# Two blocks of a network on one core: the second block's projections and gates as one stage of seven block products, kept in DRAM

## The chip, the cores and the metric

One NeuronCore of a Trainium2 chip. Its engines: TensorE (PE; weight loads are shown apart, as PEld), VectorE (DVE), ScalarE (ACT), GpSimd (POOL), and SyncE (SP), which here only issues transfers. A ScalarE row marked ACTq is a transfer that ScalarE issues. The metric is the device time of one launch, in microseconds (us), a median over runs.

## The reference, cut to what matters

`x` has 1024 tokens and 1024 features, in fp32. A first block (mLSTM, window attention, a gated convolutional feed-forward part) is followed by a second one, on which the change works:

```
xn   = rmsnorm_2(x, attn_norm_g)
proj = xn @ w_in                        # 1024 x 4864
u_pool, qkv_dil, qkv_sb, u_s5 = ...     # 512 + 2304 + 1536 + 512 columns
y_pool = pool_mixer(u_pool)             # running means over 2, 4, 8, 16 tokens, then 128x128 products
y_dil  = dilated_attention(qkv_dil)     # 3 groups of 4 heads, dilation 1, 4, 16, relative bias
y_sb   = stick_breaking_attention(qkv_sb)   # 4 heads of 128
y_s5   = s5_mixer(u_s5)                 # a state-space scan, gelu, a gated product
for bi, yb in enumerate((y_pool, y_dil, y_sb, y_s5)):
    gate   = sigmoid(xn @ w_gate[bi])   # 1024 x 1024 each
    merged = merged + gate * (yb @ w_branch[row:row + width])
x = x + merged @ w_out                  # then a feed-forward part and a last norm
```

So `xn` is multiplied by 38 column tiles of `w_in` (128 columns each) and by 32 of `w_gate`.

## The kernel before

**Dense products.** Every fp32 operand of a dense product is split into a rounded part and a rest, `hi` and `lo`; one product is three matmuls of 128x128 by 128x512: hi hi, lo hi, hi lo. Activations lie feature-major: 8 tiles of 128 features by 1024 tokens, in two halves of 512 tokens. A column tile of weights against all of `xn` takes 8 x 2 x 3 = 48 matmuls. The up and down products of both feed-forward parts save an eighth of that: they take a 2x2 block form of Winograd's, with seven block products instead of eight, at the price of sums of weights and operands before and sums of products after.

**The second block's stages.** The down product of the first block (`seven_down`, L1867) ends with the norm that makes `xn`: VectorE scales (L2053), ScalarE rounds (L1976), VectorE makes the rests (L2057). Three stages follow, each a block of its own, with a barrier at its end:

1. `pool_and_dilated` (L3132). A dense `Stream` (L2951) makes 30 column tiles: u for the pooling, q, k and v of the three dilated groups, v of the stick-breaking heads, and q, k of two of its heads. SyncE loads weights in half tiles of 256 KB (L2986), three in flight; GpSimd rounds them (L3004) and makes the rests (L3006); TensorE multiplies (L3041); ScalarE and VectorE empty the banks. v is turned from feature-major to token-major on TensorE as it comes (L3027). Beside it runs the "side" work. The relative bias is summed in the first steps and stored 12 times, once a head, from one partition to 128 skewed rows in DRAM (`bias_scratch<-xT`, 192 KB each, issued by ScalarE, L3464). SyncE reads it back as bias tiles (L3525) as soon as the four stores of a group have landed. The pooling chain runs on VectorE, with one product a group (L3266). Then the three groups, 8 blocks each: TensorE scores (L3282), VectorE bias (L3379) and maximum (L3384), ScalarE exponentials, TensorE turns (L3293) and outputs (L3305). Two groups' rows go through DRAM (`dil_scratch`) to be reordered; a mixing step (L3447, L3449) weighs the groups.
2. `stick_branch` (L3587). A second `Stream` of 8 column tiles beside 48 units of attention, one of up to 512 query columns each: logits (L3653), ScalarE's log of the remainder (L3719 to L3726), VectorE, a cast and a rest on GpSimd (L3752, L3754), products with triangular matrices that sum over later keys (L3668, L3670, L3681, L3682), the output (L3690).
3. `merge` (L4121). By a list of steps, per half of the tokens, half of the output features and branch: 8 weight tiles of the gate and 2 or 4 of the branch, 12 matmuls each (L4423); sigmoid on ScalarE (L4190), gate times product on VectorE (L4214), addition on GpSimd (L4329). The S5 scan's pieces stand at fixed steps (L4354, L4365, L4368, L4385). The gate weights are read, rounded and split once for each half of the tokens.

**What sets the order.** Each engine runs its own instruction list in the order in which it was written; semaphores tie the lists together. In stages 1 and 2 a list of booleans decides, for every engine alike, whether the next piece is the stream's or the side's:

```
def woven(order, stream, side):
    for own in order:
        next(stream if own else side, None)
```

`spread` (L3111) makes that list, an even mixture of the stream's slots (of 8 matmuls) and the side's steps.

Of the kernel before, what the change touches and what calls it, by code (L numbers as in the profile page):

```python
# [33 lines left out]
BRANCH_AT = 214976  # L34
# [221 lines left out]
def build(nc, io):  # L256
    with ExitStack() as ctx:
# [15 lines left out]
        with ExitStack() as s1:  # L273
# [12 lines left out]
            with ExitStack() as s2:  # L286
# [12 lines left out]
            branches = Stream(c, "px", branch_jobs(io), xn[0], xn[1], 2, None, at=BRANCH_AT)  # L299
            branches.ident = ident[:, :]  # L300
            down1, ahead, xn_saved, finish = seven_down(
                c, "down1", io["w_down"][0], xT, lambda k: ada[:, 40 + k, 0:1], (xT, saved[0]), xn,
                c.vec[:, 2, 96:112].rearrange("p (j k) -> p j k", j=2), (gains[:, 2, :], gains[:, 3, :]),
                (xT, saved[1]), branches, kept, up1.lead)
            down.append(down1)
            in_one_block(nc, (mix, up1, down1))
            ahead += [xn_saved, finish]
        second_block(c, io, xT, ident, ones, gains, s5, xn, hid, h, saved, branches, ahead, kept)
# [1558 lines left out]
def seven_down(c, name, w, x, gate, first, h, gain, outer, save, ahead, kept, lead):  # L1867
# [19 lines left out]
    total, weighted, r1, r12, root = (lambda half, j=j: cell(((41, 42, 43, 35, 36), (32, 33, 34, 37, HEAD))[half][j]) for j in range(5))  # L1887
# [63 lines left out]
    def scalar(act):  # L1951
# [52 lines left out]
        if h is not None:  # L2004
            for k in range(DK):
                rounding(1, k)
# [6 lines left out]
    def vector(dve):  # L2013
# [205 lines left out]
    def finish_store(act):  # L2219
        act.wait_ge(outer_made, 2 * DK)  # L2220
        act.dma_start(save[1][:, :, RIGHT], save[0][:, :, RIGHT]).then_inc(saved[1], 16)

    return Programs(sync, scalar, vector, gpsimd, tensor, split_hi, split_lo, scaled), begun, saved, (finish, finish_store)
# [632 lines left out]
SB_E = 128  # L2856
O_POOL, O_DIL, O_SB, O_S5 = 0, 512, 2816, 4352
# [11 lines left out]
def second_block(c, io, xT, ident, ones, gains, s5, xn_pair, hid, h, saved, branches, ahead, kept):  # L2869
    nc = c.nc  # L2870
    if True:
        with ExitStack() as s1:
            c.sb("xn_room", [P, 2 * DK * T], s1)
            xn_hi, xn_lo = xn_pair[0], xn_pair[1]
            yT = c.sb("yT", [P, Y_TILES, T], s1)
            w_in = io["w_in_2"][0].rearrange("(k p) n -> p k n", p=P)
            with ExitStack() as s2:
                pool_and_dilated(c, io, branches, ahead, yT, xT, ident, s2)
            c.end_stage()
            with ExitStack() as s2:  # L2880
                stick_branch(c, io, w_in, xn_hi, xn_lo, yT, xT, ident, ones, s5["u"], s2)
            c.end_stage()
            with ExitStack() as s3:
                merged, lead = merge(c, io, s5, xn_hi, xn_lo, yT, xT, s3)
        second_feed_forward(c, io, xT, ident, gains, hid, h, saved, kept, merged, lead)


def second_feed_forward(c, io, xT, ident, gains, hid, h, saved, kept, merged, lead):
# [5 lines left out]
    down2, _, _, _ = seven_down(c, "down2", io["w_down_2"][0], xT, None, (xT, saved[2]), None,  # L2894
# [1658 lines left out]
```

## Time and profile before

| | |
|---|---|
| three runs | 3680.94, 3684.49, 3688.26 us; median 3684.49 |
| span of the profiled execution, from its first to its last instruction | 3678.0 us |
| busy in the span | PE 93%, PEld 74%, DVE 54%, ACT 34%, POOL 30% |
| stage 1, 1588 to 2047 us | PE busy 440.95 of 459 |
| stage 2, 2052 to 2256 us | PE busy 195.74 of 204 |
| stage 3, 2256 to 2892 us | PE busy 603.74 of 636 |

The page gives the span of the profiled execution; launch and end around it are in the runs' times only. Busy times are sums over instructions; matmuls are pipelined, so that the mean duration of one (about 0.4 us) is longer than the pitch at which they follow one another. A line of a group gives after the bar the busy time, the mean of one instruction, and the idle time of the engine just before them with what ended it.

### The profile page before, as it was taken

Reading aid. Unit: us, or ns where it says so; the run is one execution under the profiler, and the core shown is the slowest. Engines: PE = TensorE matmul, PEld = TensorE weight load, DVE = VectorE, ACT = ScalarE, POOL = GpSimd, SP = SyncE. Lnnn points to the kernel's source line nnn. Section 1 sums busy time; section 2 is a strip of 40 time slices with the busy share of each in tenths; the row PEclk is TensorE's granted clock in tenths of the full one; section 3 lists DMA queues with packets and bytes.
Section 4 is the critical chain, followed back from the end, with each engine's and each line's share of the span. In section 5 each row is a group of like instructions: output and inputs, shape, how many; then the busy total and the mean of one; then the engine's idle time right before and its main releaser. Section 6 shows DMA issues by size and latency. Waiting matters only on the chain. (4 is left out here: it accounts for less than half of the span.)

```text
span 3678.0 us, 44316 instructions
## 1 busy us (share of the span) xinstructions
PE 3424.0 (93%) x16719; PEld 2726.2 (74%) x16719; DVE 2002.8 (54%) x2809; ACT 1251.9 (34%) x2205; POOL 1101.5 (30%) x950
## 2 busy tenths in 40 slices
PE   5799998988999999879999898999999989999998
PEld 3577777866788888767888676775777767888886
DVE  5346654556867768833335443542434466555586
ACT  3523333144333344411223354231333333222343
POOL 4122112213655510222222453551111135444111
PEclk7799999999999999989999999999999999999999
DMA  8611112032333346238111112442222423333552
GB/s 255 230 54 44 58 46 101 36 119 87 98 101 103 109 170 202 72 83 74 50 46 50 30 29 77 123 134 69 92 92 93 162 82 108 96 108 101 197 184 95
DMA packets 317982, 373.41 MB, mean 102 GB/s; under 512 B 30254, under 2 KB 225166, under 8 KB 316986
## 3 DMA queue, kind: packets, MB, share of 16 engines
q1 hardware_dynamic: 307880, 342.29, 29.3%
q10 hardware_dynamic: 3490, 11.35, 2.6%
q0 software_dynamic: 6400, 16.94, 1.8%
q8 instruction: 134, 2.20, 0.2%
q14 instruction: 78, 0.64, 0.1%
HBM read 283.58 MB, written 86.28 MB: 101 GB/s over the span
## 5 line engine op out<-in xcount | busy, mean ns | idle before, releaser
L2348 POOL TENSOR_TENSOR up_w_lo<-up_w_sum,up_w_hi 128x512 fp32r<-128x512 f32 x176 | 248.4, 1440 | 326.3 <-ACT up_w_hi L2324 324.5
L4250 DVE TENSOR_TENSOR mg_w_lo<-mg_raw,mg_w_hi 128x512 fp32r<-128x512 f32 x184 | 153.4, 836 | 208.5 <-ACT mg_w_hi L4178 208.0
L2348 POOL TENSOR_TENSOR up_w_lo<-up_raw,up_w_hi 128x512 fp32r<-128x512 f32 x132 | 201.4, 1541 | 129.3 <-ACT up_w_hi L2324 129.3
L4178 ACT CAST mg_w_hi<-mg_raw 128x512 fp32r<-128x512 f32 x184 | 115.1, 626 | 354.1 <-PE ps L4423 173.2
L1920 ACT CAST down_hi<-down_room 128x1024 fp32r<-128x1024 f32 x154 | 161.0, 1051 | 210.7 <-PE ps L2200 131.7
L1924 DVE TENSOR_TENSOR down_lo<-down_room,down_hi 128x1024 fp32r<-128x1024 f32 x154 | 192.1, 1253 | 71.4 <-ACT down_hi L1920 70.2
L3041 PE MATMUL ps<-xn_hi_at,px_w_hi 128*128 128x512 f32 x480 | 193.5, 403 | 32.5 <-PEq L1507 17.9
L2324 ACT CAST up_w_hi<-up_w_sum 128x512 fp32r<-128x512 f32 x176 | 99.7, 614 | 323.4 <-DVE up_w_sum L2337 323.4
L762 PE MATMUL ps<-h_hi,stream_hi 128*128 128x512 f32 (+1 forms) x488 | 185.3, 380 | 24.7 <-POOL stream_lo L737 17.4
L2554 PE MATMUL ps<-h_hi_at,up_w_lo 128*128 128x512 f32 x704 | 191.6, 394 | 16.0 <-POOL up_w_lo L2348 16.0
L2554 PE MATMUL ps<-h_hi_at,up_w_hi 128*128 128x512 f32 x704 | 192.9, 396 | 7.2 <-ACT up_w_hi L2324 7.2
L3041 PE MATMUL ps<-xn_hi_at,px_w_lo 128*128 128x512 f32 x480 | 191.9, 400 | 0.0
L3041 PE MATMUL ps<-xn_lo_at,px_w_hi 128*128 128x512 f32 x480 | 191.3, 399 | 0.0
L2554 PE MATMUL ps<-h_lo_at,up_w_hi 128*128 128x512 f32 x704 | 190.8, 393 | 0.0
L762 PE MATMUL ps<-h_hi,stream_lo 128*128 128x512 f32 (+1 forms) x488 | 184.7, 379 | 0.0
L762 PE MATMUL ps<-h_lo,stream_hi 128*128 128x512 f32 (+1 forms) x488 | 183.8, 377 | 0.0
L2200 PE MATMUL ps<-down_hi 128*128 128x512 f32 x616 | 167.0, 393 | 3.5 <-ACT down_hi L1920 3.5
L4329 POOL TENSOR_TENSOR xT<-xT,sig 128x512 f32<-128x512 f32 x48 | 67.6, 1408 | 342.7 <-DVE sig L4214 336.7
L2554 PEld LDWEIGHTS ps<-h_hi_at,up_w_lo 128*128 128x128 f32 x704 | 133.8, 191 | 45.4 <-POOL up_w_lo L2348 17.7
L2200 PE MATMUL ps<-down_hi,down_lo 128*128 128x512 f32 x616 | 165.5, 391 | 0.0
L2200 PE MATMUL ps<-down_lo,down_hi 128*128 128x512 f32 x616 | 165.5, 391 | 0.0
L2554 PEld LDWEIGHTS ps<-h_hi_at,up_w_hi 128*128 128x128 f32 x704 | 134.0, 191 | 37.8 <-ACT up_w_hi L2324 8.9
(598 smaller groups left out, 8018.1 us busy)
## 6 DMA issues: line engine op xcount, KB each, us to landing
up_raw<-in_w_up SPq DMA_DIRECT2D x88, 512.0 KB, 5.2
down_room<-hid_kept SPq DMA_DIRECT2D x154, 256.0 KB, 2.9
mg_raw<-in_w_gate SPq DMA_DIRECT2D x128, 256.0 KB, 2.7
hid_kept<-up_out SPq DMA_DIRECT2D x44, 512.0 KB, 3.6
down_room<-in_w_down SPq DMA_DIRECT2D x88, 256.0 KB, 4.3
px_raw<-in_w_in SPq DMA_DIRECT2D x60, 256.0 KB, 3.0
mg_raw<-in_w_branch SPq DMA_DIRECT2D x56, 256.0 KB, 2.7
wa<-in_w_ada SPq DMA_DIRECT2D x12, 1024.0 KB, 9.9
```

Source lines behind the costliest of these rows:

```text
L762: ins = nc.tensor.matmul(ps[:, self.bank + q % 2, 0:size], w[:, i % 2, k * P:(k + 1) * P], r[:, k, at:at + size], start=(x == 0), stop=(x ...
L1920: nc.scalar.copy(hi[:, u % R], both(u)).then_inc(hi_made, 1)
L1924: nc.vector.tensor_tensor(lo[:, u % R], both(u), hi[:, u % R].bitcast(F32), ALU.subtract).then_inc(rest_made, 1)
L2200: ins = nc.tensor.matmul(bank(q, j), a[:, u % R, n, j * P:(j + 1) * P], b[:, u % R, 1 - n, :], start=(k == 0 and r == 0), stop=(k == KH - ...
L2324: nc.scalar.copy(w_hi[:, s, :], source(t, i)).then_inc(hi_made, 1)
L2348: nc.gpsimd.tensor_tensor(w_lo[:, s, :], source(t, i), w_hi[:, s, :].bitcast(F32), ALU.subtract).then_inc(lo_made, 1)
L2554: ins = nc.tensor.matmul(bank(t, i), wp[:, s, k * P:(k + 1) * P], op[:, k], start=(r == 0 and k == 0), stop=(r == 2 and k == H - 1))
L3041: ins = nc.tensor.matmul(ps[:, half, :], w[:, n % 2, k * P:(k + 1) * P], x[:, 4 * kh + k, half * BANK:(half + 1) * BANK], start=(kh == 0 a ...
L4178: nc.scalar.copy(w_hi[:, s, :], w_raw[:, s, :]).then_inc(hi_ready[s], 1)
L4250: nc.vector.tensor_tensor(w_lo[:, s, :], w_raw[:, s, :], w_hi[:, s, :].bitcast(F32), ALU.subtract).then_inc(lo_ready[s], 1)
L4329: nc.gpsimd.tensor_tensor(target(i, m), target(i, m), sig[:, m, :], ALU.add).then_inc(added, 1)
```

## The change

A new stage, `project_all`, stands between the down product and stage 1. It makes all 70 column tiles that multiply `xn` (38 projections, 32 gates) in 35 pairs, each pair by seven block products of 12 matmuls. VectorE makes the weight sums and the sums of products, ScalarE rounds weights and applies sigmoid, scale or S5's order of steps, GpSimd makes the rests. The results are stored to DRAM, two tiles of 512 KB a pair. The list of pairs, the operands and TensorE's program:

```diff
+def projection_pairs(io, proj, gates, u_dram):
...
+    starts += [O_SB + 1024 + h * P for h in range(4)] + [O_SB + h * P for h in (0, 1, 4, 5, 2, 3, 6, 7)]
+    kinds = ["plain"] * len(starts)
+    kinds[SB_TILE] = kinds[SB_TILE + 1] = kinds[SB_TILE + 4] = kinds[SB_TILE + 5] = "scale"
+    tiles = [(w_in[:, :, at:at + P], kind, proj[:, i, :]) for i, (at, kind) in enumerate(zip(starts, kinds))]
+    tiles += [(w_in[:, :, O_S5 + m * P:O_S5 + (m + 1) * P], "steps", u_dram[8 * m:8 * m + 8].rearrange("g ch s k -> (g ch) s k")) for m in range(4)]
+    for b in range(N_BRANCH):
+        wg = io["w_gate_2"][0, b].rearrange("(k p) n -> p k n", p=P)
+        tiles += [(wg[:, :, m * P:(m + 1) * P], "sigmoid", gates[:, b * DK + m, :]) for m in range(DK)]
+    return [tiles[i:i + 2] for i in range(0, len(tiles), 2)]
...
+        self.ops = [(hi[:, 0:H, L], lo[:, 0:H, L]), (hi[:, H:DK, L], lo[:, H:DK, L]), (hi[:, H:DK, R], self.late_lo),
+                    (hi[:, 0:H, R], lo[:, 0:H, R])] + [(self.t_hi[:, n], self.t_lo[:, n]) for n in range(3)]
+        self.sums = {3: xn[2][:, 0:H, R], 4: self.t_sum[:, 0], 5: self.t_sum[:, 1], 6: self.t_sum[:, 2]}
...
+        self.order = [(0, 0), (0, 1), (1, 0), (1, 1)] + [(t, i) for t in range(len(pairs)) for i in range(2 if t < 2 else 0, self.N)]
...
+    def tensor(self, pe):
+        nc, H, N = self.c.nc, self.H, self.N
+        for t, i in self.order:
+            e, s = self.entry(t, i)
+            if e >= 8:
+                before, j = self.order[e - 8]
+                if j == 0:
+                    pe.wait_ge(self.p1_copied, before + 1)
+                else:
+                    pe.wait_ge(self.u_made, N * before + self.READ[j])
+            if t == 0 and i == 2:
+                pe.wait_ge(self.late_made, H)
+            elif t == 0 and i > 2:
+                pe.wait_ge(self.op_hi, self.OP_AT[i] + H)
+                if i in (3, 4):
+                    pe.wait_ge(self.op_lo, (i - 2) * H)
+                else:
+                    pe.wait_ge(self.op_lo_pool, (i - 4) * H)
+            pe.wait_ge(self.hi_made, e + 1)
+            hi, lo = self.ops[i]
+            for r, (wp, op) in enumerate(((self.w_hi, hi), (self.w_hi, lo), (self.w_lo, hi))):
+                if r == 2:
+                    pe.wait_ge(self.lo_made, e + 1)
+                for k in range(H):
+                    ins = nc.tensor.matmul(self.bank(t, i), wp[:, s, k * P:(k + 1) * P], op[:, k], start=(r == 0 and k == 0), stop=(r == 2 and k == H - 1))
+            ins.then_inc(self.used, 1)
```

SyncE loads two tiles of weights a pair (512 KB each) and stores the pair before; ScalarE's steady order in a pair, and VectorE's:

```diff
+            if more and t:
+                cast(t + 1, 1)
+            if t:
+                post(t - 1, 1)
+            if more:
+                for i in (2, 3, 4):
+                    cast(t + 1, i)
+            post(t, 0)
+            if more:
+                for i in (5, 6):
+                    cast(t + 1, i)
...
+            tt(a[:, 0, :], self.p1[:, :], self.bank(t, 1), ALU.add).then_inc(self.u_made, 1)
+            if t == 0:
+                x_scale(dve)
+            if more:
+                for which in range(3):
+                    sums_of(t + 1, which)
+            dve.wait_ge(self.used, self.place[t, 4] + 1)
+            tt(self.u2[:, :], self.p1[:, :], self.bank(t, 4), ALU.add).then_inc(self.u_made, 1)
+            dve.wait_ge(self.u_made, base + 2)
+            tt(self.u4[:, :], self.u2[:, :], self.bank(t, 3), ALU.add).then_inc(self.u_made, 1)
+            dve.wait_ge(self.u_made, base + 3)
+            tt(a[:, 1, :], self.u4[:, :], self.bank(t, 2), ALU.add).then_inc(self.u_made, 1)
+            if more:
+                sums_of(t + 1, 3)
+            dve.wait_ge(self.used, self.place[t, 5] + 1)
+            tt(self.u3[:, :], self.u2[:, :], self.bank(t, 5), ALU.add).then_inc(self.u_made, 1)
+            dve.wait_ge(self.u_made, base + 5)
+            tt(up[:, 1, :], self.u3[:, :], self.bank(t, 3), ALU.add).then_inc(self.u_made, 1)
+            dve.wait_ge(self.used, self.place[t, 6] + 1)
+            tt(up[:, 0, :], self.u3[:, :], self.bank(t, 6), ALU.add).then_inc(self.u_made, 1)
```

At the down product's end the rests of the right half of the tokens (L2057) go, and its roundings are made for four feature tiles only:

```diff
-                if k and h is not None:
+                if k and h is not None and half == 0:
```

Stages 1 and 2 lose their streams: the lists of the engines hold only the side's work, and SyncE loads u, q, k and v from DRAM. v is turned on TensorE inside the side's steps (`turn_values`, `take_values`). The part of SyncE in stage 1:

```diff
+        for g in range(2):
+            sp.dma_start(u[:, g, :], proj[:, g, :]).then_inc(u_loaded[g], 16)
...
+        for g in range(2, G):
+            sp.dma_start(u[:, g, :], proj[:, g, :]).then_inc(u_loaded[g], 16)
+        for j in range(2):
+            load_values(j)
+        sp.dma_start(kept_qk[:, 0], proj[:, 4:8, :]).then_inc(qk_loaded[0], 16)
+        load_values(2)
+        load_values(3)
+        load_bias(0)
+        load_bias(1)
+        for n in range(1, 3):
+            sp.dma_start(kept_qk[:, n], proj[:, 4 + 6 * n:8 + 6 * n, :]).then_inc(qk_loaded[n], 16)
+        for j in range(4, 8):
+            load_values(j)
+        sp.wait_ge(dsem[0]["done"], 1)
+        for r in range(4):
+            sp.dma_start(scratch[0].rearrange("(b l r) x -> r l b x", b=2, r=4)[r], o[:, 2 * r:2 * r + 2, :]).then_inc(o_stored, 16)
+        load_bias(2)
+        sp.dma_start(spare[:, 0:4, :], proj[:, SB_TILE:SB_TILE + 4, :]).then_inc(heads_loaded, 16)
+        sp.wait_ge(dsem[1]["done"], 1)
+        sp.dma_start(scratch[1].rearrange("(l a) x -> l a x", a=NB), o[:, :, :]).then_inc(o_stored, 16)
+        for j in range(8, 10):
+            load_values(j)
```

**ScalarE, head of stage 1.** Before (line numbers of the kernel before; `yT` and `dil_even` copies empty the stream's banks, L3468 is the pooling's result, `bias_scratch` a skew store):

```order
L3455 ACT_TABLE_LOAD
L3180 COPY yT<-ps 128x512 x4
L3464 DMA bias_scratch<-xT 128x1x384 x2
L3180 COPY dil_even<-ps 128x512
L3464 DMA bias_scratch<-xT 128x1x384 x2
L3468 ACTIVATE yT<-ps,vec 128x1024
```

Now, in the changed kernel's line numbers (L3644 is the skew store, L3648 the pooling's result, L3400 a turned value tile):

```order
L3635 ACT_TABLE_LOAD
L3644 DMA bias_scratch<-xT 128x1x384 x4
L3648 ACTIVATE yT<-ps,vec 128x1024
L3400 COPY yT<-ps 128x4x128
L3644 DMA bias_scratch<-xT 128x1x384 x2
L3648 ACTIVATE yT<-ps,vec 128x1024
```

The bank copies are gone; four skew stores now stand ahead of the pooling's first result, then two behind each.

**SyncE, head of stage 1.** Before (`px_raw` are the stream's weights, `bias_dil` the bias tiles):

```order
L2986 DMA px_raw<-in_w_in 128x4x128 x3
L3529 DMA xT<-in_rel_bias 32x12
L3530 DMA xT<-in_k_onehot 32x1152
L3531 DMA xT<-in_k_skewmask 4x1152
L3533 DMA pool_w<-in_pool_w 128x4x128
L3534 DMA vec<-in_k_ramp 128x32
L2986 DMA px_raw<-in_w_in 128x4x128 x17
L3525 DMA bias_dil<-bias_scratch 128x128 x16
L2986 DMA px_raw<-in_w_in 128x4x128 x14
```

Now, from the last of the small tables on (`yT` takes u, `v_tokens` a value tile of 512 KB, `kept_qk` q and k of a group, 2 MB):

```order
L3719 DMA xT<-in_k_skewmask 4x1152
L3721 DMA pool_w<-in_pool_w 128x4x128
L3722 DMA vec<-in_k_ramp 128x32
L3724 DMA yT<-proj_kept 128x1024 x2
L3713 DMA v_tokens<-proj_kept 128x1024 x2
L3727 DMA kept_qk<-proj_kept 128x4096
L3713 DMA v_tokens<-proj_kept 128x1024 x2
L3709 DMA bias_dil<-bias_scratch 128x128 x16
L3733 DMA kept_qk<-proj_kept 128x4096 x2
L3713 DMA v_tokens<-proj_kept 128x1024 x4
```

The bias loads had 17 weight loads of 256 KB before them; now they have four tiles of u (two of them further up), four of v and a group's q and k, and other projections follow.

**TensorE, a unit of stage 2.** Before (L3668 to L3690 as above, L3041 the stream):

```order
L3668 MATMUL ps<-sb_s_hi,sb_later 128x512
L3670 MATMUL ps<-sb_s_lo,sb_later 128x512
L3653 MATMUL ps<-xT 128x512
L3681 MATMUL ps<-sb_s_hi,sb_upto 128x512
L3682 MATMUL ps<-sb_s_lo,sb_upto 128x512
L3690 MATMUL ps<-sb_d,yT 128x512
L3041 MATMUL ps<-xn_hi_at,w_hi 128x512
L3041 MATMUL ps<-xn_lo_at,w_hi 128x512
L3041 MATMUL ps<-xn_hi_at,w_lo 128x512
```

Now (L3828 to L3850 are the same products):

```order
L3828 MATMUL ps<-sb_s_hi,sb_later 128x512
L3830 MATMUL ps<-sb_s_lo,sb_later 128x512
L3813 MATMUL ps<-xT 128x512
L3841 MATMUL ps<-sb_s_hi,sb_upto 128x512
L3842 MATMUL ps<-sb_s_lo,sb_upto 128x512
L3850 MATMUL ps<-sb_d,yT 128x512
L3828 MATMUL ps<-sb_s_hi,sb_later 128x512
```

Where the stream's matmuls stood between two units, the next unit follows directly.

Stage 3 no longer multiplies gates. It runs 64 units (a branch, a half of the output features, a half of the tokens, a tile of 128), each 12 or 6 matmuls; SyncE loads the gate of each as a tile of 256 KB, VectorE multiplies, GpSimd adds. Branches come in the order 0, 2, 1, 3, and the S5 pieces stand at fixed units. Inputs of S5 and the first branch weights are loaded in stage 2.

```diff
+    ORDER = (0, 2, 1, 3)
+    GROUPS, UNITS = 2 * N_BRANCH, 8 * 2 * N_BRANCH
+    IN, OUT, GLU = (0, 6, 12, 18), (9, 15, 21, 28), (33, 37, 41, 44)
...
+            sp.dma_start(gate[:, u % 4, :], gates[:, b * DK + h * M + m, n * BANK:(n + 1) * BANK]).then_inc(gate_loaded[u % 4], 16)
...
+            if u >= 4:
+                pe.wait_ge(taken, u - 3)
+            count = BRANCH_TILES[b]
+            cols = slice(m * P, (m + 1) * P)
+            for r, (wp, op) in enumerate(((w_hi, s_hi), (w_hi, s_lo), (w_lo, s_hi))):
+                for k in range(count):
+                    if m == 0 and r < 2:
+                        pe.wait_ge(lo_made if r else hi_made, max(number["w", g, k], number["y", g // 2, n, k]) + 1)
+                    last = nc.tensor.matmul(c.ps[:, 4 + m, :], wp[g % 2][:, k, cols], op[n][:, k, :],
+                                            start=(r == 0 and k == 0), stop=(r == 2 and k == count - 1))
+            last.then_inc(summed, 1)
```

## Rows read from the trace of the kernel before

**Rows 1.** Windows of the three stages: length, busy us (instructions), clock, DMA share

```profile
core 0: us, PE busy (x) PEld busy (x) DVE busy (x) ACT busy (x) POOL busy (x), PEclk, DMA share, GB/s
1588.00:2047.00 459.00, 440.95 (x2258) 358.63 (x2258) 163.55 (x295) 90.12 (x256) 113.30 (x116) 0.98 0.33 56
2052.00:2256.00 204.00, 195.74 (x824) 144.37 (x824) 83.21 (x153) 102.20 (x209) 102.00 (x128) 0.98 0.12 32
2256.00:2892.00 636.00, 603.74 (x2658) 461.31 (x2659) 263.01 (x363) 196.21 (x324) 166.39 (x190) 0.99 0.35 105
```

**Rows 2.** TensorE by line, 1588 to 2892 us: busy us, mean ns, idle before

```profile
L3041 PE MATMUL ps<-xn_hi_at,px_w_hi 128*128 128x512 f32 x480 | 193.5, 403 | 32.5 <-PEq L1507 17.9 <-ACT xT L3180 6.3 <-POOL px_w_lo L3006 3.2
...
L4423 PE MATMUL ps<-xn_hi_at,mg_w_hi 128*128 128x512 f32 x512 | 141.0, 397 | 18.9 <-ACT mg_w_hi L4178 14.6 <-PE ps L4423 4.3
...
L3041 PE MATMUL ps<-xn_hi_at,w_hi 128*128 128x512 f32 x128 | 55.3, 432 | 4.4 <-POOL w_lo L3006 3.3 <-DVE xT L3602 1.1
```

**Rows 3.** Timeline of TensorE in the up product; start, us, line, count

```profile
1001.20 1.07 PE L2554 MATMUL ps<-h_lo_at,up_w_hi 128*128 128x512 f32 x4
...
1004.83 1.07 PE L2554 MATMUL ps<-h_hi_at,up_w_lo 128*128 128x512 f32 x4
```

**Rows 4.** VectorE's groups by line at the down product's end, 1570 to 1590 us

```profile
L2057 DVE TENSOR_TENSOR xn_lo_at<-xn_plain_at,xn_hi_at 128x512 fp32r<-128x512 f32 x8 | 5.5, 690 | 0.1
```

**Rows 5.** The page's costliest groups, a weight rest on GpSimd in the up product

```profile
L2348 POOL TENSOR_TENSOR up_w_lo<-up_w_sum,up_w_hi 128x512 fp32r<-128x512 f32 x176 | 248.4, 1440 | 326.3 <-ACT up_w_hi L2324 324.5
```

**Rows 6.** Windows of the up product, its start and 100 us later

```profile
890.00:930.00 40.00, 26.55 (x83) 18.97 (x82) 35.85 (x35) 16.60 (x30) 28.48 (x17) 0.81 0.25 72
...
1000.00:1100.00 100.00, 100.00 (x443) 82.80 (x442) 71.90 (x85) 34.22 (x51) 54.38 (x36) 1.00 0.35 111
```

**Rows 7.** DMA view, 1588 to 1730 us: queues; issues (KB, us to landing)

```profile
q10 hardware_dynamic: 2768, 4.46, 53.7%
q1 hardware_dynamic: 12585, 6.26, 15.5%
...
px_raw<-in_w_in SPq DMA_DIRECT2D x20, 256.0 KB, 13.3
...
pool_w<-in_pool_w SPq DMA_DIRECT2D x1, 256.0 KB, 3.0
```

**Rows 8.** Timeline of ScalarE, issues of the skew stores (ACTq)

```profile
1636.88 1.22 ACTq L3464 DMA_DIRECT2D bias_scratch<-xT  x2
...
1685.59 7.92 ACTq L3464 DMA_DIRECT2D bias_scratch<-xT  x2
```

**Rows 9.** Window of the pooling chain, under the skew stores

```profile
1645.00:1691.00 46.00, 45.40 (x189) 35.21 (x188) 24.81 (x36) 5.37 (x7) 14.92 (x13) 1.00 0.93 64
```

**Rows 10.** Timeline of VectorE: blocks of one part, of two, and of the mixing

```profile
1789.83 0.69 DVE L3379 SCALAR_TENSOR_TENSOR yT<-ps,bias_dil 128x512 f32<-128x512 f32 x1 [3.59 <-PE ps L3282]
...
1793.19 0.18 DVE L3394 RECIPROCAL stat<-stat 128x4 f32<-128x4 f32 x1
...
1947.74 1.42 DVE L3379 SCALAR_TENSOR_TENSOR xT<-ps,bias_dil 128x512 f32<-128x512 f32 x2 [1.32 <-PE ps L3282]
...
1952.36 0.18 DVE L3394 RECIPROCAL stat<-stat 128x4 f32<-128x4 f32 x1
...
2012.83 0.42 DVE L3447 TENSOR_TENSOR o_dil<-o_dil 128x256 f32<-128x256 f32 x1
...
2015.24 0.82 DVE L3447 TENSOR_TENSOR o_dil<-o_dil 128x256 f32<-128x256 f32 x1
```

**Rows 11.** Timeline of the stick-breaking loop, logits and the last step of a unit

```profile
2111.76 1.02 PE L3653 MATMUL ps<-xT 128*128 128x512 f32 x2
...
2116.22 1.28 POOL L3754 TENSOR_TENSOR sb_s_lo<-sb_t,sb_s_hi 128x512 fp32r<-128x512 f32 x1
```

**Rows 12.** Windows in the pool stage and at the stick stage's end

```profile
1730.00:1740.00 10.00, 5.51 (x15) 4.03 (x14) 1.55 (x3) 2.56 (x9) 0.00 (x0) 0.68 0.49 126
2246.00:2256.00 10.00, 6.70 (x21) 3.13 (x19) 4.51 (x7) 5.81 (x11) 3.77 (x4) 1.00 0.19 39
```

More of the change, by code:

```diff
@@ L3099, in woven @@
-def woven(order, stream, side):
-    for own in order:
-        next(stream if own else side, None)
-    for rest in (stream, side):
-        for _ in rest:
-            pass
 def spread(n_stream, n_side):
@@ new lines, in project_all, with _, pool_and_dilated @@
+def project_all(c, px, begun, left_saved, x_scale):
+    with c.nc.Block() as block:
+        @block.sync
+        def _(sp):
+            next(begun)
+        @block.scalar
+        def _(act):
+            px.scalar(act, left_saved)
+        @block.vector
+        def _(dve):
+            px.vector(dve, x_scale)
+        @block.gpsimd
+        def _(pool):
+            px.gpsimd(pool)
+        @block.tensor
+        def _(pe):
+            px.tensor(pe)
+def pool_and_dilated(c, io, proj, yT, spare, ident, s2):
@@ L4161, in target @@
+    def target(u):
+        _, _, h, n, m = unit(u)
         return spare[:, h * M + m, n * BANK:(n + 1) * BANK]
     def sync(sp):
-        for j, (i, k, g, _, _) in enumerate(steps):
-            (_, h, b), s = segs[i], j % 2
-            if j >= 2:
-                sp.wait_ge(lo_ready[s], 2 * (j // 2))
-            cols = slice(h * BANK, (h + 1) * BANK)
-            rows = gate[b, k * P:(k + 1) * P, cols] if g else wide[(y_tile[b] + k) * P:(y_tile[b] + k + 1) * P, cols]
-            sp.dma_start(w_raw[:, s, :], rows).then_inc(loaded[s], 16)
@@ L4203, in vector @@
[L4203 to L4216 removed]
+        todo = list(enumerate(weights))[2:]
@@ new lines, in vector, with split_lo, take, turn_inputs @@
+    def vector(dve):
+        tt = nc.vector.tensor_tensor
+        def split_lo(i):
+            src, hi, lo = spots(splits[i])
+            dve.wait_ge(hi_made, i + 1)
+            tt(lo, src, hi.bitcast(F32), ALU.subtract).then_inc(lo_made, 1)
+        def take(u):
+            dve.wait_ge(summed, u + 1)
+            dve.wait_ge(gate_loaded[u % 4], 16 * (u // 4 + 1))
+            dst = target(u) if u < 16 else gate[:, u % 4, :]
+            tt(dst, c.ps[:, 4 + u % 4, :], gate[:, u % 4, :], ALU.mult).then_inc(taken, 1)
+        def turn_inputs(m, part):
@@ L4348, in tensor @@
+        for u in range(UNITS):
+            for k in range(4):
+                if IN[k] + 6 <= u <= IN[k] + 8:
+                    make_state(k, u - IN[k] - 6)
+            pool.wait_ge(taken, u + 1)
+            if u < 16:
+                pool.nop().then_inc(added, 1)
+            else:
+                pool.wait_ge(added, u - 15)
+                nc.gpsimd.tensor_tensor(target(u), target(u), gate[:, u % 4, :], ALU.add).then_inc(added, 1)
     def tensor(pe):
         def inputs(m):
-            pe.wait_ge(in_loaded[m], 16 * (S5_L + 2))
+            if m:
+                pe.wait_ge(in_loaded[m], 32)
+                pe.wait_ge(x_made, 4 * m)
@@ L4431, in merge, with gate_rows @@
-    last_gate = [max(j for j, step in enumerate(steps) if step[2] and j % 2 == s) for s in range(2)]
+        def gate_rows(t):
+            if t == 0:
+                pe.wait_ge(y_back, 16 * 4)
+                pe.wait_ge(x_made, 16)
+                pe.wait_ge(s5_out, 4)
+            else:
+                pe.wait_ge(glu_done, t)
+            pe.wait_ge(glu_loaded[t % 2], 32 * (t // 2 + 1))
+            for part in range(2):
+                for n in range(2):
+                    for k in range(4):
+                        last = nc.tensor.matmul(c.ps[:, 2 * part + n, :], cs[:, t % 2, part, k, :],
+                                                y_rows[:, k, n * BANK:(n + 1) * BANK], start=(k == 0), stop=(k == 3))
+            last.then_inc(glu_summed, 1)
```

1109 lines of the change are left out of this document (565 added, 544 removed).

## The prediction

> **What bounds the kernel now.** I read the page's busy shares first: TensorE is busy for 93% of the span, so the kernel is a chain of matmuls and a change is worth what it does to TensorE's work and to its idle time. Then I took the windows of the three stages that the change rewrites [rows 1]: 1588 to 2047 us (pool and dilated), 2052 to 2256 (stick-breaking), 2256 to 2892 (merge), in all 459 + 204 + 636 and the gap of 5 between two blocks = 1304 us, of which TensorE idles 18, 8 and 32. It idles so little because in each stage a dense product fills it: the grouped view of TensorE's lines [rows 2] has 3 x 480 matmuls of the first stream, 3 x 128 of the second and 3 x 512 of the gates, 3360 in all. The timeline of a full stretch gives their pitch: 16 matmuls from 1001.20 to 1004.83 us [rows 3], 0.2267 us each. So dense products are 1440 x 0.2267 = 326, 87 and 348 us of the three stages; what is left on TensorE without them is 441 - 326 = 114, 196 - 87 = 108 and 604 - 348 = 255 us. Those three numbers decide: the change takes away 420 dense matmuls, and takes away from the first two stages the work that covered the latencies of the other engines.
>
> **The change, part by part.** I sum the new region, and set it against 1304.
>
> *End of the down product.* Eight rests of 0.69 us on VectorE go from its tail [rows 4]; a cast still follows the last scaling there. I take -4.5 us (0 to -5.5).
>
> *The product stage.* 35 pairs x 7 blocks x 12 matmuls = 2940; x 0.2267 = 666.5 us, 95 less than 3360 would take. This holds if nothing else is slower per pair than 84 x 0.2267 = 19.0 us. GpSimd makes 7 rests a pair, at 1.44 us in the up product, which has the same form [rows 5]: 10.1 us. VectorE makes 4 sums and 7 combining operations of 512 columns: 11 x 0.69 (the duration of [rows 4]) = 7.6. ScalarE makes 7 casts and a copy. SyncE moves 2 MB; at the 19 us of a pair that is 110 GB/s, what the up product moves while TensorE is busy for 100.00 of 100 us [rows 6]. So TensorE bounds it.
>
> *Its start.* Only the first products can start at once; the operands of blocks 3 to 6 need 36 VectorE operations and casts. The up product starts in the same way, and there 83 matmuls run from 890 to 930 us [rows 6]: 83 x 0.2267 = 18.8 of 40 us, 21 lost. I take 20 (14 to 27).
>
> *Its drain.* The last combination, a sigmoid, two stores of 512 KB and the barrier: 7.5 us, an estimate.
>
> *Pool and dilated, front.* In the new kernel the twelve skew stores stand at the head of ScalarE's work and SyncE has 6.4 MB of kept projections to load ahead of the first bias. In the trace the queue that ScalarE issues on held 53.7% of the sixteen engines from 1588 to 1730 us [rows 7]; 76 us, of which 7 belong to the copy of x, so the stores need 69 us of all engines, 5.7 each. ScalarE itself gets stuck on them: the first pair issues in 1.22 us, a late pair in 7.92 [rows 8]. And loads suffer: 256 KB of weights land in 13.3 us there, a tile of the same size (pool_w) in 3.0 [rows 7]. Before, all that lay beside the stream: TensorE was busy for 45.40 of 46 us under the stores, though the DMA engines were taken to 0.93 [rows 9]. Now the dilated groups wait for their bias, which waits for its stores and then stands on SyncE's queue behind the 6.4 MB. (Behind the waiting bias loads stand the q and k of the later groups and four value tiles; nothing needs them before the first group is under way.) If the stores did not gate, the pooling chain would: VectorE's 25 us in that window [rows 9], 10 before it and 2 behind, 37 us. If the loads keep the slowdown 13.3 / 3.0 = 4.4, the bias comes behind everything: 10 + 69 + 25 = 104 (23 us being q1's 15.5% of the window, for about as many MB, and a landing). I take 92, near the upper end since the row nearest to the case, px_raw, shows it, less what 4-KB rows save against those of 512 bytes.
>
> The Trainium skill ("DMA: Bandwidth & Descriptors", section "Queues, rings and completion order") says that each DMA engine takes turns between the queues that have work, a whole packet at a time. The trace agrees in the 13.3 against 3.0 us [rows 7]; by that rule SyncE's large packets would gain against the stores, and the front would fall below my 92.
>
> *Pool and dilated, groups.* A block of the dilated attention with two key parts runs on VectorE from 1947.74 to 1952.54, 4.80 us; one with a single part from 1789.83 to 1793.37, 3.54 [rows 10]. With the stream gone nothing else stands between, and TensorE's scores for the next block are issued early. 11 x 4.80 + 13 x 3.54 = 99; heads and tails of three groups 3 x 6.5 (an estimate: the exponentials and turns that only the first and last block show), the ten value tiles now copied here some 4: 122 us.
>
> *Pool and dilated, mixing.* Eight blocks of 2.41 us (2012.83 to 2015.24 [rows 10]) = 19, and some 13 (an estimate) for the stored rows to come back, the weights and the turn at the end: 32. The stage: 92 + 122 + 32 = 246, against 459 before. Removing 326 us of dense work shortens it by 213 only: 113 us that were hidden come to light. The gap to the next block stays 5.
>
> *Stick-breaking.* A unit's chain is logits, ScalarE, VectorE, GpSimd, TensorE. The logits of a unit of 512 columns start at 2111.76 and its last step on GpSimd ends at 2116.22 + 1.28 = 2117.50 [rows 11]; with the product that waits for it 6.0 us, and two units are under way at a time. That loop, not TensorE, is what paces the stage without a stream: 12 pairs x 6.0 + 12 narrower x 4.4 (scaled by their columns) = 125, and 9 for the lead and the tail: 134. TensorE's own 108 is the lower bound (112 with a lead); the upper is 160, all pairs wide.
>
> *Merge.* Without gates TensorE has 255 us here; GpSimd keeps its additions, VectorE and ScalarE lose 128 rests and casts of gate weights, and gates come as tiles of 256 KB, one in 2.7 us of matmuls. I take 256 (240 to 281: idle time of the S5 steps gone, or 25 us more of it than now).
>
> Sum: -4.5 + 666.5 + 20 + 7.5 + 246 + 5 + 134 + 256 = 1330.5, against 1304: 26.5 us slower. The profiled execution's span of 3678.0 lies 6.5 below the median 3684.5; carried to the median the forecast is 3711 us.
>
> **The rivals.**
> B, faster: the stores do not gate. SyncE's loads pass them, and ScalarE's issue blocks nothing that is waited for; then the front is 37 instead of 92: 3711 - 55 = 3656 us. For it: the first group needs only its own four stores, 10 + 4 x 5.7 = 33 us. Against it: 13.3 us for 256 KB [rows 7], with 6.4 MB ahead of the bias.
> C, slower: TensorE's clock falls in the branch stages. From 1730 to 1740 us TensorE was busy for 5.51 of 10 us, and the granted clock was 0.68; from 2246 to 2256 it was busy for 6.70, without a stream, at 1.00 [rows 12]. The new stages have 114 of 246 and 108 of 134 us. If half of these 222 us ran at 1.2 GHz, they would take another 111, of which the other engines' steps hide about half: some 50 us, 3761. [...] The Trainium skill ("TensorE: Matmul & The Clock Gate", section "HAM oscillation — how this bites in real kernels") tells the same of bursts of matmuls between waits; the low window of [rows 12] agrees, the later one does not.
> D, slower still than the forecast: the product stage is not bound by TensorE. Stores and loads of 2 MB a pair, or ScalarE's order of casts and sigmoids, cost 1 us a pair: +35, 3745. Against it: the 100.00 of [rows 6].
>
> **How the numbers follow.** The forecast's own case A has 0.50, with 3690 to 3735 as its own range (the bounds of start, stick stage and merge, added in quadrature); B 0.25, C 0.13, D 0.12. What a measurement of this kernel can tell from no change is 0.2%, 7.4 us: faster is below 3677, slower above 3692. Of A, 0.02 lies below, 0.09 within, 0.39 above; of B 0.23 and 0.02; C and D lie above. Faster 0.25, same 0.11, slower 0.64. The range from 3652 to 3758 leaves out the lower part of B (0.1) and the upper one of C (0.1).
>
> **What will show it.** In the changed profile: a stage of some 694 us with TensorE full from 30 us after its start (D wrong); in the next block TensorE idle for about 90 us under the bias stores with the DMA share near 0.9 (B wrong), or dilated scores within 45 us (A wrong); 3.5 and 4.8 us a block on VectorE; 3.0 us a unit in the stick stage; 256 us of merge; a granted clock near 1.0 in both branch stages (C wrong). The prediction fails if the front lies below 60 us, or if the products need over 20 us a pair.

## The result, and the profile after

The changed kernel takes 3800.03 us (four runs, 3794.11 to 3802.32), the kernel before 3685.58: a ratio of 1.0304, 95% interval 1.029 to 1.0319. It is slower, as forecast, but by 114 us where the forecast had 26 and its range ended at 73 above.

The span is 3800.5 us against 3678.0, and the mean granted clock of TensorE 0.926 against 0.965. The spans differ by 122.5 us where the medians differ by 114, since the profiled execution of the kernel before lies 6.5 us under its median; stages are compared by the profiled executions. The windows of the new stages answer to [rows 1], in the same columns; the last four rows are stretches of the product stage's start, of its middle (they answer to [rows 6]), and of the third dilated group:

```profile
1588.00:2295.00 707.00, 677.20 (x2940) 557.85 (x2940) 299.65 (x429) 216.23 (x342) 352.90 (x253) 0.98 0.34 105
2295.00:2392.00 97.00, 23.53 (x62) 11.31 (x62) 24.42 (x39) 7.76 (x9) 0.00 (x0) 0.57 0.92 97
2392.00:2557.00 165.00, 124.81 (x732) 110.71 (x732) 85.75 (x164) 62.19 (x211) 0.00 (x0) 0.62 0.23 79
2557.00:2595.00 38.00, 7.61 (x26) 4.23 (x25) 20.03 (x54) 3.73 (x7) 0.79 (x1) 0.50 0.18 56
2595.00:2733.00 138.00, 118.19 (x440) 72.12 (x440) 76.96 (x147) 97.76 (x201) 72.48 (x97) 0.96 0.27 50
2733.00:3018.00 285.00, 261.77 (x1124) 191.29 (x1125) 124.81 (x181) 46.78 (x71) 104.15 (x71) 0.90 0.45 133
...
1590.00:1650.00 60.00, 36.86 (x125) 28.06 (x125) 53.66 (x59) 18.17 (x33) 47.85 (x24) 0.78 0.25 72
2000.00:2100.00 100.00, 100.00 (x443) 82.81 (x442) 41.20 (x63) 37.61 (x57) 50.20 (x38) 1.00 0.33 106
2520.00:2530.00 10.00, 10.00 (x55) 9.45 (x55) 6.18 (x11) 4.65 (x14) 0.00 (x0) 0.50 0.01 2
...
2493.00:2545.00 52.00, 42.77 (x280) 38.15 (x276) 29.97 (x50) 20.80 (x64) 0.00 (x0) 0.63 0.12 42
```

| stage | forecast, us | measured | |
|---|---|---|---|
| end of the down product | -4.5 | 0 | the new stage starts where the old one did |
| products, start, drain | 694 | 707 | +13 |
| pool and dilated, front | 92 | 97 | +5 |
| dilated groups | 122 | 165 | +43 |
| mixing and the gap | 37 | 38 | +1 |
| stick-breaking | 134 | 138 | +4 |
| merge | 256 | 285 | +29 |
| sum | 1330.5 | 1430 | +99.5 |

The border at 2392 lies 4.6 us before the first bias addition of the groups (2396.60), the one at 2557 lies 2.6 us before their last output (2559.63). By those two events the front took 102 us and the groups 163.

Read the clock column of the first six rows. Where the dense product runs it is 0.98 and TensorE is full (443 matmuls in 100 us, 0.2257 each). In the groups it is 0.62, in the merge 0.90; those two stages hold 72 of the 99.5 us. The ten microseconds from 2520 are worth a stop: TensorE's records fill 10.00 of 10 us there, and it is granted 0.50.

The front came out nearly as worked out. The DMA view from 2295 to 2400 us, with the columns of [rows 7]:

```profile
q10 hardware_dynamic: 1728, 2.36, 68.2%
q1 hardware_dynamic: 4391, 8.03, 22.2%
...
kept_qk<-proj_kept SPq DMA_DIRECT2D x3, 2048.0 KB, 11.9
v_tokens<-proj_kept SPq DMA_DIRECT2D x6, 512.0 KB, 13.2
bias_scratch<-xT ACTq DMA_DIRECT2D x12, 192.0 KB, 26.1
...
bias_dil<-bias_scratch SPq DMA_DIRECT2D x16, 64.0 KB, 12.1
```

And the timelines of the same stretch, the issues of ScalarE and SyncE and the first bias addition, then two neighbouring blocks of the third group on VectorE and the last output of the groups (they answer to [rows 8] and [rows 10]):

```profile
2316.12 16.10 ACTq L3644 DMA_DIRECT2D bias_scratch<-xT  x2
...
2342.32 7.44 ACTq L3644 DMA_DIRECT2D bias_scratch<-xT  x1
...
2338.85 59.35 SPq L3709 DMA_DIRECT2D bias_dil<-bias_scratch  x16
...
2396.60 0.69 DVE L3557 SCALAR_TENSOR_TENSOR yT<-ps,bias_dil 128x512 f32<-128x512 f32 x1 [56.57 <-DMA bias_dil<-bias_scratch]
...
2500.82 1.42 DVE L3557 SCALAR_TENSOR_TENSOR xT<-ps,bias_dil 128x512 f32<-128x512 f32 x2
...
2508.42 1.42 DVE L3557 SCALAR_TENSOR_TENSOR xT<-ps,bias_dil 128x512 f32<-128x512 f32 x2 [1.35 <-PE ps L3454]
...
2559.21 0.42 DVE L3579 TENSOR_TENSOR o_dil<-ps,stat 128x256 f32<-128x256 f32 x1 [3.57 <-PE ps L3477]
```

One skew store after another holds ScalarE's issue for 7.4 us; SyncE needs 59 us to issue the bias loads of two groups, beside the stores that are still under way; VectorE stands for 56.57 us until those of the first group land. That is the front. The block in the third group is another matter: 7.60 us from 2500.82 to 2508.42, where VectorE's own steps took 4.80 in the kernel before [rows 10].

### The profile page after: what moved, and what is told of

It is laid out like the page before. It is cut to its first block and busy times, and to the rows that moved or that the text cites. A ratio compares the mean times of both kernels' runs of the same rounds, so it can differ in the third digit from the quotient of the medians.

```text
span 3800.5 us, 43875 instructions
## 1 busy us (share of the span) xinstructions
PE 3394.8 (89%) x16299; PEld 2708.0 (71%) x16299; DVE 2114.9 (56%) x3000; ACT 1292.7 (34%) x2249; POOL 1240.5 (33%) x931
## 5 line engine op out<-in xcount | busy, mean ns | idle before, releaser
L3256 POOL TENSOR_TENSOR px_w_lo<-px_w_sum,px_w_hi 128x512 fp32r<-128x512 f32 x140 | 205.2, 1498 | 287.1 <-ACT px_w_hi L3110 287.1
L3110 ACT CAST px_w_hi<-px_w_sum 128x512 fp32r<-128x512 f32 x140 | 79.9, 617 | 312.7 <-DVE px_w_sum L3190 312.6
L3296 PE MATMUL ps<-xn_hi_at,px_w_hi 128*128 128x512 f32 x560 | 152.9, 395 | 30.7 <-ACT px_w_hi L3110 16.0
L2164 POOL TENSOR_TENSOR down_room<-down_room 128x512 f32<-128x512 f32 x20 | 40.3, 2015 | 391.7 <-ACT down_room L1959 390.6
L3256 POOL TENSOR_TENSOR px_w_lo<-px_raw,px_w_hi 128x512 fp32r<-128x512 f32 x105 | 135.8, 1309 | 84.8 <-ACT px_w_hi L3110 84.8
L3296 PE MATMUL ps<-xn_hi_at,px_w_lo 128*128 128x512 f32 x560 | 152.3, 394 | 5.2 <-POOL px_w_lo L3256 5.2
```

Source lines behind the costliest of these rows:

```text
L2164: step(nc.gpsimd.tensor_tensor(total(half), sq(half, k - 1) if k == (H + 1 if half else 1) else total(half), sq(half, k), ALU.add))
L3110: nc.scalar.copy(self.w_hi[:, s, :], self.source(t, i)).then_inc(self.hi_made, 1)
L3256: nc.gpsimd.tensor_tensor(self.w_lo[:, s, :], self.source(t, i), self.w_hi[:, s, :].bitcast(F32), ALU.subtract).then_inc(self.lo_made, 1)
L3296: ins = nc.tensor.matmul(self.bank(t, i), wp[:, s, k * P:(k + 1) * P], op[:, k], start=(r == 0 and k == 0), stop=(r == 2 and k == H - 1))
```

## The experiments

Each is the changed kernel with one edit, run once, unless said otherwise. Spans are compared with 3800.5, the longest of the changed kernel's four (the shortest is 3792.3), so that a gain of under some 8 us says nothing by itself. For the groups the time from the first bias addition to the last output decides. It is 163.0 us in the changed kernel, and 161.3 in the run with S5's outputs later, which leaves the groups as they are; the 165 us of the expectations are the window.

**One and two extra matmuls a block.** They go into an unused bank, only to keep TensorE at work (fp32, 128x128 by 128x512). The second stands behind the scores of the next block.

```diff
                 turn(b)
+                keep_busy(1)
```

> One extra fp32 matmul of 128x128 by 128x512 into an unused bank behind each block's turn in the dilated groups (24 in all); nothing reads it. In the changed kernel the three groups take 165 us (2392 to 2557), with granted clocks of 0.50 to 0.84, where 122 were forecast. Theory 1 (the groups are slow because TensorE runs at 1.2 GHz most of the time): the clock there rises to 0.9 or more and the groups take 125 to 140 us, the whole 25 to 40 us less than 3800. Theory 2 (the chain of steps over VectorE, ScalarE and TensorE in each block sets the pace at either clock): the clock rises and the groups still take 155 or more; the whole within 10 us of 3800. If the clock stays as it is, the groups get some 10 to 25 us longer and the run tells nothing between the two.

> As the run with one extra matmul, with a second one behind each block's scores (48 in all). Theory 1 (clock): if one extra matmul is too little to keep the clock up, two do, and the groups take 130 to 145 us at a clock of 0.95 or more. Theory 2 (chain of steps): groups 160 to 190 us at a high clock, since the extra 0.9 us a block come on top.

Measured: spans of 3788.7 and 3785.4, -12 and -15. The groups take 153.7 and 148.9 us, against 163.0. The third group's window in the run with one (first fence) and with two (second):

```profile
2493.00:2545.00 52.00, 40.31 (x291) 32.30 (x291) 30.44 (x52) 23.50 (x72) 0.00 (x0) 0.86 0.07 24
```

```profile
2493.00:2545.00 52.00, 46.49 (x326) 33.63 (x326) 31.51 (x55) 23.59 (x71) 0.00 (x0) 0.96 0.06 22
```

The clock rises from 0.63 to 0.86 and 0.96, and only 9 and 14 us come back, less than the first theory has and more than the second. It looked more like the second, the chain of steps. But with two extra matmuls TensorE is busy for 46 of 52 us. Summed over its lines in the groups, TensorE's own products take 95 us instead of 134, and the extra ones 55: what the clock gave, the extra work took. The pair does not decide.

**Half of TensorE's products in the groups; no value turns; both.** The first leaves out two of four heads in scores, turns and outputs, the second the turns of the six value tiles that are turned inside the groups, and with them the loads of the last two; the other engines do what they did.

```diff
-                    for h in range(DH):
+                    for h in range(2):
...
-    DIL_TURNS = [{}, {2: 4, 4: 5}, {1: 6, 2: 7, 4: 8, 5: 9}]
+    DIL_TURNS = [{}, {}, {}]
```

> In the dilated groups TensorE does half of each block's products (two of four heads in scores, turns and outputs); the other engines do all they did, on stale banks. At 1.2 GHz TensorE's work per block is then what the full work would be at 2.4 GHz. Theory 1 (TensorE at 1.2 GHz is the bound of a block): the groups fall from 165 to 125 to 140 us. Theory 2 (the steps of VectorE and ScalarE with their waits, at the order in which they are written, set the pace): the groups stay at 152 or more. The run with one extra matmul a block, 12 us faster at a clock near 1, lies between.

> The six value tiles that are turned inside the dilated groups are left out (the first four, turned in the pooling steps, stay), so later groups multiply stale values. In the changed kernel a block with a turn takes 9.6 us where its neighbours take 6.9 to 7.7. Theory 1 (the turns stand in the loop of a block, and I had put them at 4 us for all ten): the groups take 15 to 22 us less, the whole 3778 to 3785. Theory 2 (they lie in TensorE's slack and the slow blocks are slow for the clock): less than 6 us.

> Both of the two: half of TensorE's products in the groups, and no value turns inside them. Theory 1 (clock and turns are all that the groups have over the forecast of 122 us): the groups take 118 to 130 us. Theory 2 (the loop over the engines costs more than the busy time of VectorE that I had counted): they take 138 us or more.

Measured: spans of 3773.4 (-27), 3788.2 (-12) and 3754.0 (-46). The groups take 134.9, 152.3 and 121.7 us, against 163.0: -28, -11 and, with both, -41. The run without turns falls between its two theories; the other two agree with their theory 1. VectorE in the run with both: the first bias addition, two of the one-part group, two of the third, and the last output; then TensorE's window in the third group:

```profile
2396.06 0.69 DVE L3557 SCALAR_TENSOR_TENSOR yT<-ps,bias_dil 128x512 f32<-128x512 f32 x1 [57.24 <-DMA bias_dil<-bias_scratch]
...
2455.37 0.69 DVE L3557 SCALAR_TENSOR_TENSOR yT<-ps,bias_dil 128x512 f32<-128x512 f32 x1
...
2458.94 0.69 DVE L3557 SCALAR_TENSOR_TENSOR yT<-ps,bias_dil 128x512 f32<-128x512 f32 x1
...
2489.78 1.42 DVE L3557 SCALAR_TENSOR_TENSOR xT<-ps,bias_dil 128x512 f32<-128x512 f32 x2 [0.21 <-PE ps L3454]
...
2494.61 1.42 DVE L3557 SCALAR_TENSOR_TENSOR xT<-ps,bias_dil 128x512 f32<-128x512 f32 x2
...
2517.35 0.42 DVE L3579 TENSOR_TENSOR o_dil<-ps,stat 128x256 f32<-128x256 f32 x1 [1.87 <-PE ps L3477]
```

```profile
2475.00:2506.00 31.00, 20.75 (x106) 17.15 (x106) 24.64 (x43) 18.33 (x59) 0.00 (x0) 0.50 0.01 2
```

3.57 and 4.83 us a block: the forecast's 3.54 and 4.80; and 121.7 us for the groups: the forecast's 122. And this at a granted clock of 0.50. There the half of the products keeps TensorE busy for 80 us (summed over its lines in the groups); all of them, in the kernel before and beside the stream, for 88. So half the products at 1.2 GHz take about the time of all of them at 2.4. The forecast's reckoning of a block by VectorE was sound and its condition was not met: with the granted clock at 0.62, TensorE's in-order work, together with the turned value tiles, is longer than VectorE's. Theory 1 holds in that TensorE's work sets the pace, and the reading of the first two runs falls. That the full clock alone would do the same is reckoned from the 80 and 88 us; no run has it without extra matmuls.

**The bias row stored by way of DRAM.** One store of the rows to DRAM, then the twelve stores read them from there.

```diff
+        act.dma_start(off_dram[:, :, :], off).then_inc(off_stored, 16)
+        act.wait_ge(off_stored, 16)
...
-act.dma_start(skewed[ORDER[n], h:h + 1], off[h:h + 1, ORDER[n], :].unsqueeze(1).to_broadcast([1, P, SKEW])).then_inc(skew_stored[n], 16)
+act.dma_start(skewed[ORDER[n], h:h + 1], bass.AP(off_dram.tensor, (h * 3 + ORDER[n]) * SKEW, [[0, 1], [0, P], [1, SKEW]])).then_inc(skew_stored[n], 16)
```

> The twelve skew stores read the bias row from DRAM (one small store of the rows first) instead of from one SBUF partition; what lands in DRAM is the same. Theory 1 (the front of the pool stage, 95 us from the stage's start to the first bias addition of the groups, waits for stores that are slow because one partition feeds all of them, 7.4 us each): the stores take under 2 us each and the front falls to 40 to 55 us, the whole by 40 to 55 us. Theory 2 (the 6.4 MB of loads ahead of the bias, or the pooling chain, set the front): the front stays above 80 us. Theory 3 (the form of the destination, 128 rows of 1536 bytes, is what is slow): the stores still take 5 us or more each and nothing changes by more than 15 us.

Measured: span 3740.3, -60. The DMA view from 2295 to 2345 us, the first bias addition, and the window up to it:

```profile
kept_qk<-proj_kept SPq DMA_DIRECT2D x3, 2048.0 KB, 12.3
...
bias_scratch<-off_dram ACTq DMA_DIRECT2D x12, 192.0 KB, 4.9
...
bias_dil<-bias_scratch SPq DMA_DIRECT2D x16, 64.0 KB, 2.0
```

```profile
2338.31 0.69 DVE L3558 SCALAR_TENSOR_TENSOR yT<-ps,bias_dil 128x512 f32<-128x512 f32 x1 [1.41 <-PE ps L3455]
```

```profile
2297.00:2339.00 42.00, 22.74 (x62) 11.13 (x62) 25.11 (x40) 7.86 (x9) 0.00 (x0) 0.65 0.84 281
```

The stores land in 4.9 us instead of 26.1, the bias loads in 2.0 instead of 12.1, while q and k, 2 MB a load, land as before (12.3, 11.9). The first addition comes 41 us after the stage's start instead of 102; VectorE's pooling, 25 of these 42 us, now sets it. The source in one partition was what was slow, since the destination and the issuing engine are the same: one store after another at 7.43 us each is 192 KB at 26.5 GB/s. The Trainium skill ("SBUF — State Buffer", section "Door 1: The DMA port swizzle") gives about 27 GB/s for what a single port of SBUF carries, and eight partitions share one; the trace agrees with 26.5.

**S5's outputs later in the merge.**

```diff
-    IN, OUT, GLU = (0, 6, 12, 18), (9, 15, 21, 28), (33, 37, 41, 44)
+    IN, OUT, GLU = (0, 6, 12, 18), (11, 17, 23, 30), (35, 38, 41, 44)
```

> In the merge the four outputs of the S5 scan stand two units later (11, 17, 23, 30 instead of 9, 15, 21, 28) and the first two gated products too (35, 38). In the changed kernel TensorE waits there for GpSimd's states, 17 us in four waits of up to 8.3 us, and the merge takes 290 us. Theory 1 (those waits and the clock that falls behind them are what the merge has over the 256 us forecast): the waits fall below 5 us and the merge by 12 to 30 us. Theory 2 (the pace is set by loads and splits elsewhere; the wait moves on): the merge changes by less than 6 us.

Measured: span 3766.8, -34. TensorE's groups in the merge, of the changed kernel (first fence) and of this run (second); below them a window of the changed kernel behind the longest of its waits, and the merge of this run:

```profile
L4628 PE MATMUL ps<-mg_s_hi,mg_w_hi 128*128 128x512 f32 x224 | 68.6, 423 | 4.6 <-ACT mg_s_hi L4447 4.6
...
L4592 PE MATMUL ps<-s_room,s_cp 64*128 64x127 f32 x128 | 18.6, 438 | 0.0
L4589 PE MATMUL ps<-s_chunk,s_room 128*128 128x128 f32 x64 | 18.0, 431 | 16.9 <-POOLq L4556 16.9
```

```profile
L4628 PE MATMUL ps<-mg_s_hi,mg_w_hi 128*128 128x512 f32 x224 | 65.0, 405 | 5.2 <-ACT mg_s_hi L4447 5.2
...
L4592 PE MATMUL ps<-s_room,s_cp 64*128 64x127 f32 x128 | 11.4, 297 | 0.0
L4589 PE MATMUL ps<-s_chunk,s_room 128*128 128x128 f32 x64 | 11.0, 294 | 0.0
```

```profile
2840.00:2850.00 10.00, 10.00 (x49) 8.05 (x50) 0.00 (x0) 1.02 (x1) 0.11 (x1) 0.50 0.18 54
```

```profile
2733.00:2984.00 251.00, 242.71 (x1128) 176.14 (x1128) 125.08 (x182) 47.01 (x71) 104.64 (x72) 0.99 0.52 151
```

The 16.9 us in which TensorE waited for GpSimd's state (L4589) are gone. So are as many more: the small products L4592 and L4589 fall from 36.6 to 22.4 us with the same counts; most of the rest comes off the other products. In the changed kernel the clock fell to 0.50 behind the wait, with TensorE's records at 10.00 of 10 us; here it is 0.99 over the whole merge, which takes 251 us, within the 256 forecast. Four waits of up to 8 us, 17 in all, had cost twice their length.

**The last scalings later at the start of the product stage.**

```diff
             tt(a[:, 0, :], self.p1[:, :], self.bank(t, 1), ALU.add).then_inc(self.u_made, 1)
-            if t == 0:
-                x_scale(dve)
...
             if more:
                 sums_of(t + 1, 3)
+            if t == 0:
+                x_scale(dve)
...
```

> At the start of the product stage VectorE makes the eight last scalings of the down product (13 us, 1.69 us each beside GpSimd's rests) ahead of the weight sums of the second pair; here they come behind those sums, and SyncE's copy of x behind the loads of the fourth pair. Theory 1 (those 13 us, which I had not counted, are why the stage takes 707 us where 694 were forecast): the stage takes 6 to 13 us less, the whole 3787 to 3794. Theory 2 (VectorE's work beside GpSimd is slowed as a whole, each operation up to twice its time alone, and the start waits for all of it in any order): less than 4 us.

Measured: span 3801.3, nothing gained. VectorE's groups from 1588 to 1650 us of the changed kernel, GpSimd's in the same stretch, VectorE's of this run, and the changed kernel's steady stage (2000 to 2100 us):

```profile
L2012 DVE SCALAR_TENSOR_TENSOR xT<-xT,vec,down_room 128x512 f32<-128x512 f32 x8 | 13.0, 1691 | 0.0
L3200 DVE TENSOR_TENSOR px_late_lo<-xn_plain_at,xn_hi_at 128x512 fp32r<-128x512 f32 x4 | 5.8, 1499 | 0.0
L3204 DVE TENSOR_TENSOR xn_plain_at<-xn_plain_at,xn_hi_at 128x512 f32<-128x512 f32 x4 | 5.8, 1497 | 0.0
...
L3190 DVE TENSOR_TENSOR px_w_sum<-px_raw 128x512 f32<-128x512 f32 x4 | 2.7, 683 | 1.0 <-PEq L1509 1.0
```

```profile
L3256 POOL TENSOR_TENSOR px_w_lo<-px_w_sum,px_w_hi 128x512 fp32r<-128x512 f32 x8 | 23.1, 2913 | 8.3 <-ACT px_w_hi L3110 8.3
```

```profile
L2012 DVE SCALAR_TENSOR_TENSOR xT<-xT,vec,down_room 128x512 f32<-128x512 f32 x8 | 13.6, 1766 | 0.0
L3201 DVE TENSOR_TENSOR px_late_lo<-xn_plain_at,xn_hi_at 128x512 fp32r<-128x512 f32 x4 | 5.8, 1497 | 0.0
```

```profile
L3190 DVE TENSOR_TENSOR px_w_sum<-px_raw 128x512 f32<-128x512 f32 x11 | 7.6, 688 | 24.0 <-PE ps L3296 24.0
...
L3256 POOL TENSOR_TENSOR px_w_lo<-px_w_sum,px_w_hi 128x512 fp32r<-128x512 f32 x23 | 31.9, 1418 | 50.7 <-ACT px_w_hi L3110 50.7
```

This agrees with theory 2: the order made no difference, and VectorE is busy from 1590 on for 54 of 60 us in the changed kernel and for 56 in this run. Sixteen of its operations on two SBUF operands take 1.5 to 1.7 us there (the scalings, L3200 and L3204), though others take 0.68, and eight of GpSimd's rests take 2.9; in the steady stage it is 0.69 and 1.4. The Trainium skill ("SBUF — State Buffer", section "SBUF: two separate sides") says that VectorE with two SBUF operands and GpSimd take turns on a shared port, a whole instruction each; the trace agrees with those pairs of durations, though no run here removed GpSimd's part to show it.

**What the edits give together.** Three edits (bias row, S5 outputs, one extra matmul), three rounds; then five (also the scalings, extra matmuls in fewer blocks, a third of the mixing's multiplications on GpSimd), five rounds.

> The three edits that gained together: the bias row stored by way of DRAM (-60 us alone), S5's outputs two units later (-33), one extra matmul a block (-12). If they act on separate stretches the sum is -105, 3695 us, within 3685 to 3705; if the extra matmul gained only where the cold front went before, 3700 to 3712. Against the kernel before that is 0 to 0.7% slower, so that the product stage's 95 us of TensorE time are still more than eaten by what the streams had hidden.

> The three edits of the combined run (3699.5 us), with the extra matmuls only in the third group and in the last three blocks of the first two, the scalings of the product stage behind the second pair's sums, and a third of the mixing's multiplications on GpSimd, which is idle there. If each gives what its row promises (scalings -6 to -13, mixing 8 x 0.42 = -3 to -5, extra matmuls -2 to -4), 3678 to 3690, the same as the kernel before (3687) or up to 0.25% faster; if the starts overlap, 3690 to 3697.

Measured: 3699.5 us, a ratio to the kernel before of 1.0035 (1.0023 to 1.0048); and 3697.45, 1.0027 (1.0018 to 1.0036). The first is what the single edits promised. The second misses its 3678 to 3690 and ends at the edge of its poorer case: the further edits gave 2 us, nothing that can be told. Of 114 us lost, some 100 came back, and no version here beats the kernel before; both intervals lie above 1.

## Why the forecast was right in sign and wrong in size

- *The products and what they save.* Right: 2940 matmuls with TensorE full at the pitch forecast. Their start cost 32 us instead of 20: 125 matmuls (28 us) in the 60 us from 1590. The term was carried over from the up product's start [rows 6], and the eight scalings that stand among VectorE's operations here, 13 us, were not counted. That they are what it lacks is not shown: no run takes them away.
- *The front.* Right in what holds it: 92 forecast, 97 measured (102 to the first bias addition). ScalarE's queue held the engines for 68.2% of 105 us, 72 where 69 were reckoned. Rival B did not come about, and SyncE's loads did not gain enough on the stores to bring the front below 92. Why the stores are slow the forecast did not say; the bias row's run shows it, and there the front is nearly rival B's, 41 us for 37.
- *Groups.* This is the step that failed: "With the stream gone nothing else stands between". It took VectorE's 4.80 and 3.54 us for the block. TensorE stood between. With the granted clock at 0.62 its products cost 28 us beyond VectorE's steps (what leaving half of them out gave back), and the value turns, put at 4 us for all ten, take 11 to 13 for the six inside the groups. That is the 41 us by which the groups (163) exceed the forecast (122).
- *Rival C* came about in part, inside the likeliest case: in the groups TensorE is busy for 125 of 165 us, and the granted clock is 0.62 all the same; in the stick stage it stayed at 0.96. The rows that spoke for the rival and against it [rows 12] were single stretches of 10 us.
- *Mixing and stick-breaking.* Right within 1 and 4 us. A block of the mixing takes 2.41 us, as forecast, and eight units of the stick stage take 20.1 (2642.31 to 2662.44) where the forecast's numbers give 20.8: a loop taken from its dependent steps [rows 11], not from an engine's busy time, came out. But TensorE is busy for 118 of the stick stage's 138 us, and no run shows which of the two sets the pace.
- *Merge.* Mis-sized: 285 instead of 256, 4 us above its upper bound. TensorE's own work was right (251 us once the waits went). The sum had no wait for S5's states, only its bound had one, and that the clock falls behind each wait was in neither.
- *The range.* The bounds of start, stick stage and merge, added in quadrature, give 3683 to 3748, not 3690 to 3735; 3800 lies above both.

## What to carry to other kernels

A dense stream beside latency-bound work does two things, and the second is easily missed: it fills waits, and it keeps up the clock of the small products around it (granted 0.98 in the old first stage [rows 1], 0.62 in the groups without the stream). Before taking one away, reckon each stage without it as a loop of dependent steps, with TensorE's small products at the lower clock, and set the sum against the matmuls saved. Here, at 0.50, an output or a turn took TensorE twice its time beside the stream, a score one and a half times. A store that read one partition 128 times went at 26.5 GB/s and held up the bias loads; by way of DRAM it was no bottleneck.

## What the runs showed of the hardware that was not expected

TensorE's records can fill a stretch completely and the granted clock stay at 0.50: 10.00 of 10 us from 2520, in scores, outputs and turns, products of 64 or 128 columns. One further 128x512 product a block brought the same group to 0.86, two to 0.96. Stores of 192 KB from a single partition ran at 26.5 GB/s, one after another, and beside them loads of 64 KB landed in 12.1 us instead of 2.0.
